# Beginning of a one-core mLSTM / attention / MoE block: per-tile first norm, shared halves, and the products around the router

## What is computed

```python
h = layer_norm(concat([pad, meta, x]), ln_in_g, ln_in_b)
proj = h @ w_in
xm, o_pre, i_pre, f_pre, qa, ka, va, ga, gb = split(proj)
y_m = mlstm_branch(xm, o_pre, i_pre, f_pre, ...)
y_a = diff_attn_branch(qa, ka, va, ...)
merged = sigmoid(ga) * (y_m @ w_branch_m) + sigmoid(gb) * (y_a @ w_branch_a)
h = layer_norm(DN_ALPHA * h + merged @ w_out, ln1_g, ln1_b)
probs = softmax(h @ w_router)
# top group of 4 experts, then top 2 experts in it, weights w normalised
for e in range(16):
    y += combine[:, e:e+1] * ((silu(h @ w_gate[e]) * (h @ w_up[e])) @ w_down[e])
h = layer_norm(DN_ALPHA * h + y, ln2_g, ln2_b)
```

## Time and profile before

| what | value |
|---|---|
| median of three runs | 827.0 us (826.32, 827.0, 827.8) |
| profiled execution, its own time | 827.67 us |
| its span | 825.9 us |
| PE busy in the span | 774.0 us (94%) |
| DVE, ACT, POOL busy | 358.1, 240.7, 25.3 us |
| HBM read | 249.91 MB, 304 GB/s over the span |

### The profile page before, as it was taken

One profiled execution on the slowest core, in us unless ns is written; L12 is line 12 of the kernel. 1 busy time (PEld: TensorE's weight loads), 2 busy tenths in 40 slices (PEclk: granted clock), 3 DMA queues, 4 the chain that ended last, 5 costly groups with the idle time before them and its releaser, 6 DMA issues.

```text
span 825.9 us, 12669 instructions
## 1 busy us (share of the span) xinstructions
PE 774.0 (94%) x4496; PEld 470.1 (57%) x4497; DVE 358.1 (43%) x780; ACT 240.7 (29%) x523; POOL 25.3 (3%) x51
## 2 busy tenths in 40 slices
PE   4999999999999999998999999889999999998993
PEld 3998679999889999882333333333333333332330
DVE  6777446654665787735323213220223122311225
ACT  2554423444766655431110111011110111011100
POOL 2003000000001000000000000000000000000001
PEclk9999999999999999989999999999999999999997
DMA  8965050553105334995999999999999999999992
GB/s 255 388 239 204 0 204 2 203 200 134 76 1 204 135 125 160 394 405 207 428 425 430 428 428 427 430 428 428 406 431 428 430 426 428 429 428 426 431 424 94
DMA packets 36764, 251.30 MB, mean 304 GB/s; under 512 B 5921, under 2 KB 13170, under 8 KB 23426
## 3 DMA queue, kind: packets, MB, share of 16 engines
q1 hardware_dynamic: 34416, 250.76, 73.9%
q10 hardware_dynamic: 2322, 0.21, 0.2%
HBM read 249.91 MB, written 1.05 MB: 304 GB/s over the span
## 4 chain that ended last, share of the span: by engine, by line
PE 72%; DMA 18%; DVE 4%; ACT 2%; issue 2%; POOL 1%; SPq 1%; DVEq 0%; POOLq 0%; ACTq 0%
PE ps L1952 27%; DMA raw<-in_w_up_e_dram 9%; DMA raw<-in_w_down_e_dram 9%; PE ps L1617 8%; PE ps L1619 7%; PE ps L1618 7%; PE ps L1905 3%; PE ps L1913 2%; PE ps L1920 2%; PE ps L1673 1%; PE ps L1669 1%; PE ps L1729 1%; PE ps L1868 1%; PE ps L1592 1%; PE ps L1870 1%
## 5 line engine op out<-in xcount | busy, mean ns | idle before, releaser
L1617 PE MATMUL ps<-hi_h,whi 128*128 128x256 f32 (+1 forms) x448 | 129.8, 290 | 3.3 <-DVE wlo L983 3.2
L1619 PE MATMUL ps<-hi_h,wlo 128*128 128x256 f32 (+1 forms) x448 | 127.4, 284 | 0.0
L1618 PE MATMUL ps<-lo_h,whi 128*128 128x256 f32 (+1 forms) x448 | 127.3, 284 | 0.0
L1952 PE MATMUL ps<-raw,hid 128*64 128x512 f32 x512 | 114.3, 596 | 7.8 <-DMA raw<-in_w_down_e_dram 7.1
L1952 PE MATMUL ps<-raw,xg 128*64 128x512 f32 x512 | 115.0, 599 | 6.8 <-DMA raw<-in_w_gate_e_dram 3.1
L983 DVE TENSOR_TENSOR wlo<-raw,whi 128x512 fp32r<-128x512 f32 x144 | 93.4, 690 | 45.3 <-ACT whi L688 42.7
L1617 PEld LDWEIGHTS ps<-hi_h,whi 128*128 128x128 f32 x448 | 84.5, 189 | 7.9 <-DVE wlo L983 4.3
L688 ACT CAST whi<-raw 128x512 fp32r<-128x512 f32 (+1 forms) x144 | 83.2, 618 | 13.2 <-PE ps L1619 11.9
L1544 DVE TENSOR_TENSOR gs<-ps,gsig 128x512 f32<-128x512 f32 x16 | 11.1, 691 | 173.9 <-ACT gsig L930 173.1
L1619 PEld LDWEIGHTS ps<-hi_h,wlo 128*128 128x128 f32 x448 | 84.5, 189 | 0.0
L1618 PEld LDWEIGHTS ps<-lo_h,whi 128*128 128x128 f32 x448 | 84.4, 188 | 0.0
(11 more groups left out here) (321 smaller groups left out, 1015.3 us busy)
## 6 DMA issues: line engine op xcount, KB each, us to landing
raw<-in_w_down_e_dram SPq DMA_DIRECT2D x32, 2048.0 KB, 18.4
raw<-in_w_gate_e_dram SPq DMA_DIRECT2D x16, 2048.0 KB, 22.1
raw<-in_w_up_e_dram SPq DMA_DIRECT2D x16, 2048.0 KB, 24.3
gate_x<-in_w_gate_e_dram SPq DMA_DIRECT2D x16, 2048.0 KB, 20.7
raw<-in_w_in_dram SPq DMA_DIRECT2D x28, 1024.0 KB, 9.1
up_x_right<-in_w_up_e_dram SPq DMA_DIRECT2D x16, 1024.0 KB, 27.2
...
raw<-in_w_branch_m_dram SPq DMA_DIRECT2D x4, 1024.0 KB, 8.3
```

The costliest lines, as they stand in the source:

```text
L1617: mm(o, w1, hi[:, k, c0:c0 + n], start=(k == 0), stop=False)
L1618: mm(o, w1, lo[:, k, c0:c0 + n], start=False, stop=False)
L1619: last = mm(o, w2, hi[:, k, c0:c0 + n], start=False, stop=(k == KB - 1))
L1952: last = mm(ps[r0:r0 + SLOTS, bank_no, :], lhs[:, k % 4, k // 4, :], w[:, k % 2, 512 * c:512 * c + 512], start=(k == 0), stop=(k == KB - 1))
```

## The change

On SP, the short loads (`wif`, gate biases, gain and bias by slot, lambda vectors) that ACT issued in the beginning stand on SP's queue, behind the four XM quarters and ahead of `rows_in` and the OG weights; the wait for the first XM quarter there is gone. Sixteen loads of 512 bytes fill a block-diagonal tile `diag` ahead of the "out" weights, after POOL has zeroed it. On POOL, rstd is made for tiles 0 and 1, then for tile 2. On ACT, tile 1 is normalised there, the narrow masks are made first, the odd k of `hfull` are made there, and `wif` is split behind the XM stream. On DVE, tiles are taken one after another, the even k of `hfull` stay, with four buffers, and the `wif` and lambda work also stands behind the XM stream. The residual's four steps come one block later. On PE, 16 fills stand ahead of the transposes, and XM's first block waits for `lo_h` k by k. In the router, the logit products take 128 columns (the 16 router columns eight times), four products of 512 columns replace the 16 of 128, and fills are 2, 4 and 3 in three places instead of 10 in one. Some tiles (`rt`, `mask`, `passed` and others) have other addresses. The hunks stand in the order SP, POOL, ACT, DVE, PE.

```diff
         sp.wait_ge(s.x_in1, 16)
         for m, what in enumerate(MATRICES):
             if what == OG:
-                sp.wait_ge(raw_in[0][0], 16)
+                with nc.allow_non_contiguous_dma(reason="a few short vectors"):
+                    sp.dma_start(wif[:], w_in[0, :, 2048:2056].rearrange("(k p) c -> p k c", p=P)).then_inc(s.wif_in, 16)
+                    sp.dma_start(gate_bias[:, 0:1], b_i.rearrange("a h -> h a")).then_inc(s.gb_in, 16)
+                    sp.dma_start(gate_bias[:, 1:2], b_f.rearrange("a h -> h a")).then_inc(s.gb_in, 16)
+                    for tile, v in ((gain4, ln1_g), (bias4, ln1_b)):
+                        sp.dma_start(tile[:], v[0].rearrange("(c i a) -> i c a", c=2, a=4)).then_inc(s.gain4_in, 16)
+                for j, v in enumerate((lam_q1, lam_q2, lam_k1, lam_k2)):
+                    sp.dma_start(lamv[:, j, :], v[0].partition_broadcast(P)).then_inc(s.lam_in, 16)
                 for j, v in enumerate((ln_in_g, ln_in_b)):
                     sp.dma_start(rows_in[:, j, :], v.partition_broadcast(P)).then_inc(s.rows_in_in, 16)
...
+            if what == "out":
+                sp.wait_ge(s.diag_zero, 2)
+                for r0, v in ((0, ln1_g), (32, ln1_b)):
+                    for k in range(KB):
+                        sp.dma_start(diag[r0 + k:r0 + k + 1, P * k:P * k + P], v[0:1, P * k:P * k + P]).then_inc(s.diag_in, 16)
...
+        pool.wait_ge(s.var_ready, 2)
+        pool.tensor_tensor(rstd[:, 0:2], ve[:, 0:2], minus_half[:, 0:2], ALU.pow).then_inc(s.rstd_ready, 1)
         pool.wait_ge(s.var_ready, 3)
-        pool.tensor_tensor(rstd[0:META, 0:1], ve[0:META, 0:1], minus_half[0:META, 0:1],
-                           ALU.pow).then_inc(s.rstd_ready, 1)
-        pool.tensor_tensor(rstd[:, 1:3], ve[:, 1:3], minus_half[:, 1:3], ALU.pow).then_inc(s.rstd_ready, 1)
+        pool.tensor_tensor(rstd[:, 2:3], ve[:, 2:3], minus_half[:, 2:3], ALU.pow).then_inc(s.rstd_ready, 1)
...
+        pool.wait_ge(s.s_done, AH)
+        pool.memset(diag[:], 0.0).then_inc(s.diag_zero, 1)
+        pool.memset(row_sel[:], 0.0).then_inc(s.diag_zero, 1)
+        pool.wait_ge(s.diag_zero, 2)
+        pool.memset(row_sel[0:KB, 0:1], 1.0).then_inc(s.diag_zero, 1)
+        pool.memset(row_sel[32:32 + KB, 1:2], 1.0).then_inc(s.diag_zero, 1)
+        pool.wait_ge(s.diag_zero, 4)
...
-        with nc.allow_non_contiguous_dma(reason="a few short vectors"):
-            for tile, v in ((gain4, ln1_g), (bias4, ln1_b)):
...
-        for k in range(KB):
-            act.wait_ge(s.h_full, k + 1)
-            act.copy(hi_h[:, k, :], hfull[:, k % 2, :]).then_inc(s.h_hi, 1)
+        act.wait_ge(s.consts, 1)
+        for narrow, wide in ((ident_b, ident), (late_b, late), (ahead_b, ahead), (before_b, before)):
+            act.copy(narrow[:], wide[:]).then_inc(s.masks_ready, 1)
+        act.wait_ge(s.nmr0_ready, 1)
+        act.activation(xt[:, 1, :], xt[:, 1, :], ACT.Identity, bias=nmr0[:], scale=rstd[:, 1:2]).then_inc(s.x1_ready, 1)
...
+        def full_half(k):
+            act.wait_ge(s.ht_t, k + 1)
+            if k >= HB:
+                act.wait_ge(s.h_lo, k - HB + 1)
+            act.activation(hfull[:, k % HB, :], ps[:, 4 + k % 4, 0:S], ACT.Identity, bias=chan[:, C_LNB + k:C_LNB + k + 1],
+                           scale=chan[:, C_LNG + k:C_LNG + k + 1]).then_inc(s.h_odd, 1)
+        def high_half(k):
+            act.wait_ge(s.h_odd if k % 2 else s.h_even, k // 2 + 1)
+            act.copy(hi_h[:, k, :], hfull[:, k % HB, :]).then_inc(s.h_hi, 1)
+        act.wait_ge(s.chan_ready, 1)
+        for k in range(0, KB, 2):
+            full_half(k + 1)
+            high_half(k)
+            high_half(k + 1)
+        stream(XM, OG)
         act.wait_ge(s.wif_in, 16)
...
         act.copy(wif_hi[:, :, 0:MH], wif[:, :, MH:2 * MH]).then_inc(s.wif_split, 1)
         act.copy(wif_hi[:, :, 32:32 + MH], wif[:, :, 0:MH]).then_inc(s.wif_split, 1)
-        stream(XM, OG)
         act.wait_ge(s.lam_sum, 1)
         act.activation(lams[:, 2:4], lams[:, 0:2], ACT.Exp).then_inc(s.lam_exp, 1)
...
+        rows = (META, P, P)
+        def tile_stats(j):
+            n = rows[j]
             dve.wait_ge((s.x_in0, s.x_in1, s.x_in2)[j], 16)
             for c in range(2):
                 own(dve.bn_stats(stats[0:n, j, c, :], xt[0:n, j, 512 * c:512 * c + 512]))
...
+        def tile_mean(j):
+            own(dve.bn_aggr(mv[0:rows[j], j, :], stats[0:rows[j], j, :, :]))
+        def tile_var(j):
+            dve.tensor_scalar(ve[0:rows[j], j:j + 1], mv[0:rows[j], j, 1:2], EPS, None, ALU.add).then_inc(s.var_ready, 1)
+        def tile_norm(j):
+            n = rows[j]
             dve.tensor_scalar(xt[0:n, j, :], xt[0:n, j, :], mv[0:n, j, 0:1], rstd[0:n, j:j + 1],
                               ALU.subtract, ALU.mult).then_inc(s.xn_ready, 1)
+        tile_stats(0)
+        tile_stats(1)
+        own.settle()
+        tile_mean(0)
+        tile_mean(1)
+        own.settle()
+        dve.wait_ge(s.consts, 1)
+        tile_var(0)
+        tile_var(1)
+        tile_stats(2)
+        dve.wait_ge(s.rstd_ready, 1)
+        dve.scalar_tensor_tensor(out=nmr0[:], in0=mv[:, 1, 0:1], scalar=-1.0, in1=rstd[:, 1:2], op0=ALU.mult,
+                                 op1=ALU.mult).then_inc(s.nmr0_ready, 1)
+        own.settle()
+        tile_mean(2)
+        own.settle()
+        tile_var(2)
+        tile_norm(0)
         dve.wait_ge(s.rows_t, 1)
-        dve.tensor_copy(chan[:], ps[:, 7, 0:81]).then_inc(s.chan_ready, 1)
+        dve.tensor_copy(chan[:], ps[:, 3, 0:81]).then_inc(s.chan_ready, 1)
+        dve.wait_ge(s.rstd_ready, 2)
+        tile_norm(2)
         dve.wait_ge(s.chan_ready, 1)
         own(dve.tensor_scalar(chan[:, C_AG:C_AG + 1], chan[:, C_AG:C_AG + 1], 1.0 - LAM_INIT, None, ALU.mult))
+        def full_half(k):
+            dve.wait_ge(s.ht_t, k + 1)
+            dve.tensor_scalar(hfull[:, k % HB, :], ps[:, 4 + k % 4, 0:S], chan[:, C_LNG + k:C_LNG + k + 1],
+                              chan[:, C_LNB + k:C_LNB + k + 1], ALU.mult, ALU.add).then_inc(s.h_even, 1)
         def low_half(k):
             dve.wait_ge(s.h_hi, k + 1)
-            dve.tensor_tensor(lo_h[:, k, :], hfull[:, k % 2, :], hi_h[:, k, :].bitcast(F32),
+            dve.tensor_tensor(lo_h[:, k, :], hfull[:, k % HB, :], hi_h[:, k, :].bitcast(F32),
                               ALU.subtract).then_inc(s.h_lo, 1)
-        for k in range(KB):
-            dve.wait_ge(s.ht_t, k + 1)
-            if k >= 2:
-                dve.wait_ge(s.h_lo, k - 1)
-            dve.tensor_scalar(hfull[:, k % 2, :], ps[:, k % 4, 0:S], chan[:, C_LNG + k:C_LNG + k + 1],
-                              chan[:, C_LNB + k:C_LNB + k + 1], ALU.mult, ALU.add).then_inc(s.h_full, 1)
-            if k:
-                low_half(k - 1)
-        low_half(KB - 1)
...
+        full_half(0)
+        full_half(2)
+        for k in range(0, KB, 2):
+            low_half(k)
+            low_half(k + 1)
+            if k + HB < KB:
+                dve.wait_ge(s.h_lo, k + 1)
+                full_half(k + HB)
         def residual(blk, odd):
-            n = blk - 2
+            n = blk - 3
             if n not in range(2 * TT):
                 return
             t, add = n % TT, n // TT
                 dve.wait_ge(s.hres_scaled, t + 1)
                 dve.tensor_tensor(hres[:, t, :], hres[:, t, :], rows_in[:, 1, :], ALU.add).then_inc(s.hres_ready, 1)
             else:
-                dve.wait_ge(s.xn_ready, t + 2)
+                dve.wait_ge(s.xn_ready, 2)
+                dve.wait_ge(s.x1_ready, 1)
                 dve.tensor_tensor(hres[:, t, :], xt[:, t + 1, :], rows_in[:, 0, :], ALU.mult).then_inc(s.hres_scaled, 1)
         stream(XM, OG, residual)
+        dve.wait_ge(s.wif_split, 2)
+        for a, b in ((0, MH), (32, 0)):
+            own(dve.tensor_tensor(wif_lo[:, :, a:a + MH], wif[:, :, b:b + MH],
+                                  wif_hi[:, :, a:a + MH].bitcast(F32), ALU.subtract))
+        own.settle()
+        dve.sem_inc(s.wif_split, 1)
+        dve.wait_ge(s.lam_in, 64)
+        own(dve.tensor_tensor(lamp[:], lamv[:, 0:2, :], lamv[:, 2:4, :], ALU.mult))
+        own.settle()
+        dve.tensor_reduce(lams[:, 0:2], lamp[:], AX.X, ALU.add).then_inc(s.lam_sum, 1)
+        dve.wait_ge(s.masks_ready, 4)
...
-        pe.transpose(ps[:, 7, 0:81], crow[:], ident[0:81, 0:81]).then_inc(s.rows_t, 1)
-        pe.wait_ge(s.xn_ready, 3)
+        pe.transpose(ps[:, 3, 0:81], crow[:], ident[0:81, 0:81]).then_inc(s.rows_t, 1)
+        keep_warm(2, 16)
+        pe.wait_ge(s.xn_ready, 2)
+        pe.wait_ge(s.x1_ready, 1)
         for k in range(KB):
             if k >= 4:
-                pe.wait_ge(s.h_full, k - 3)
+                pe.wait_ge(s.h_odd if k % 2 else s.h_even, (k - 4) // 2 + 1)
             c = slice(P * k, P * k + P)
-            pe.transpose(ps[:, k % 4, 0:META], xt[0:META, 0, c], ident[0:META, 0:META])
-            pe.transpose(ps[:, k % 4, META:META + P], xt[:, 1, c], ident[:])
```

(35 more changed lines are left out.)

104 lines of the change are left out of this document (46 added, 58 removed).

## The result

The median of four executions went from 827.4 us (826.32 to 832.14) to 817.95 us (816.67 to 819.34); the ratio is 0.9875, 95% interval 0.9832 to 0.9918. Taken from the 827.0 us that I reckoned with, the ratio gives 816.7 us, where I had forecast 819.5 with a range from 817.3: faster, as forecast, but by more than the range allowed. The miss is 0.6 us, less than the interval of the ratio leaves open (813.1 to 820.2 us). The ratio is that of the two means, 817.98 and 828.32 us, and the execution of 832.14 alone lifts the second: without it the mean is 827.04, the ratio about 0.989, and 817.9 us would lie within the range.

What follows compares the result with a forecast made beforehand. The end was taken to follow the first expert unit at a fixed time, with PE the long pole before it. 5.4 - 1.5 + 3.6 = 7.5 us gain gave 819.5 us against the 827.0 median; range 817.3 to 823.5.

Steps and rivals of the forecast that it cites:

- What bounds the kernel: Whole kernel: the end lies a fixed time behind the first expert unit; the DMAs' empty stretch shrinks by nearly 4 us.
- The beginning: Before XM's second block: early fills, faster transposes and work shared with ACT gain 5.4 us, bounds 3.6 and 6.0.
- Behind the XM stream: Between the last XM block and second OG split: moved wif and lambda steps lose 1.5 us, bounds 0.7 and 2.2.
- SP's queue: Loads in the beginning: nine short loads delay the OG weights by up to 5.4 us; taken as no loss.
- (c): OG weights land late behind the short loads, 1 to 2 us of PE wait at 41 us: 821.0; chance 0.08.
- (d): Short loads hold SP's queue, PE loses 9 us or more at the OG weights: 828.5 or later; chance 0.04.
- The router: Logits to rank product: wide products and fewer fills gain 3.6 us if TensorE's clock stays high; bounds -0.1 and 4.3.
- Behind the ranks all is as before: After the rank product: pick, gather and first expert unit stay unchanged; no gain or loss counted.
- may do so again: First expert unit's products, at 0.50 granted clock at 375 us before, may run low again; no time counted.
- Rival (a): Router: the clock falls all the same, gain 0 to 0.6 us instead of 3.6: 822.8; chance 0.14.
- Rival (b): Beginning: the clock falls during the transposes behind the early fills, cost 1.7 us: 821.2; chance 0.16.
- Rival (e): Fills low until 14.2 us, block 1 only 3.6 us earlier, clock also falls at router: 824.9; chance 0.08.

Runs made afterwards that it cites:

- the second profile: Profiled execution of the changed kernel, run again without any edit beside the kernel before: 816.50 us.
- the first experiment: The changed kernel run again without any edit, beside the kernel before on one chip: 816.50 to 819.89 us, ratio 0.9847.

## Why the prediction was right, and where it was wrong

**What bounds the kernel: right.** The end follows the first expert unit at a fixed distance, 443.6 us before and after. The empty stretch of the DMAs was to shrink by nearly 4 us; it went from about 372 to 381 us to about 368.3 to 373.

**The beginning, 5.4 us: right in size, by some luck.** XM's second block starts at 20.16 us, forecast 20.2, before 25.71: 5.5 us. Errors inside cancel. The fills began at 6.85 us, not 7.4, and took 6.21 us, not 5.6, so that they ended at 13.0 us as forecast; in the second profile they ended at 12.1. The three transposes of a k took 0.53 us, not 0.41, since they start 0.16, 0.16 and 0.21 us apart and not 0.135, and all 24 took 4.1 us, not 3.2. But the first block's eight k then followed each other at 0.38 us, as if all halves had been there, where I had PE wait for `lo_h` until 19.7; and the second block followed the first without a gap, where I had it wait for the split of its weights. In the second profile it starts at 19.20 us, 6.5 us earlier than in the profile of before, past my bound of 6.0.

**Behind the XM stream, -1.5 us: right.** Measured -1.7 (54.7 against 53.0 us), of which the steps inside the stream give 1.4 back in one profile.

**SP's queue, 0: right.** The OG weights are issued from 20.28 us and land in 13.0 us; no engine waits for them. The price of the issues was too low: the first two short loads took 2.83 and 3.39 us on the queue, and all nine 9.2 us, not 5.4. It cost nothing. Rivals (c) and (d) fall.

**The router, 3.6 us: right in kind, too small.** The first half's logits start 3.76 us earlier than before (355.11 and 351.35), the rank product 8.44: 4.7 us, past my upper bound of 4.3. Set back by those 3.76 us, the spreading starts at 360.28, where I had the logits end at 360.85, and the mask is written at 364.16, where I had it at 364.7: the wide logits took 2.05 against 1.96 us, and the idle time ahead of them was filled. From its start to the fills the spreading took 3.43 us, not 3.6; four fills held the rank product up for 0.89, not 1.1. That is 0.95, and the last 0.1 I had rounded away (3.6 for 3.7). I had priced records by their full duration, where the pace is the distance between two starts. And the reason was named too broadly: I credited dense, wide products and the filled gap together. With the fills in place neither width alone does anything, and in one profile the two fills in the wait for `ht` and six fills fewer behind the spreading do nearly all of it; whether the fills do it without a wide product in every execution stays open.

**The step that failed.** In the sum it is the router term, 3.6 us where 4.7 were measured. In the range it is another: "Behind the ranks all is as before". I took the one profiled execution of before for the kernel, and priced nothing for executions that differ from it. The arithmetic of my low end was wrong too: the three bounds as I wrote them down give 6.0 - 1.2 + 4.3 = 9.1 us and 817.9; with the bound of 0.7 that I had given for the XM stream they give 9.6 and 817.4. So 817.3 left out nothing as unlikely together; it was all of them together, and the time came out below.

What the runs show in its place is a clock that does three things that vary between executions of one kernel: how long the early fills run low (4.47 to 5.95 us for all of them in the old beginning, 5.29 to 6.39 in the new), where it falls at the router (without the two fills 12.5, 14.1 or 15.65 us from turn to rank product), and whether the gate products run low (7.09 or 8.46 to 8.78 us). The terms of the sum, compared profile with profile (827.67 and 819.34, both with low gate products), give 8.3 us against 7.5. From there to the 10.3 us of the ratio it is 2.0 us. Of these, 1.3 come from the one of four executions before in the group near 832, which the router's fills abolish. The other 0.7 come from the executions after that are faster than the profiled one (816.67 and 817.03 us), less the same before: by the two profiles of the changed kernel such an execution has the gate products at full clock (1.6 us) and shorter early fills (1.0 us). In the first experiment, where nine of 17 executions of before are in the upper group, the ratio was 0.9847. The earlier trace rows showed two of these falls; that the second need not come ("may do so again", I wrote) had a price of 1.4 us, and it belonged in the range, below the forecast.

**Rival (a)**, the clock falls at the router all the same, did not happen in any profile with the two fills; without them, in the kernel with the new beginning alone, it did, 10 us long. In eight executions of the kernel before with the two fills it may have (their mean clock says so). **Rival (b)**: the clock did not fall behind the early fills. **Rival (e)** did not come either: the fills ended at 13.3 us at the latest. The Trainium skill, "TensorE: Matmul & The Clock Gate", Part 4, PE-mode transpose, says that transposes don't count as busy for the clock gate in the way that products do. The traces agree as far as they don't raise it: 24 of them in a row, without fills, ran at 421 and 474 ns to the last, and before as well. But 24 transposes in 4.1 us right behind the fills did not let it fall either, and the first XM products took 289 to 299 ns in the mean. The 1.7 us that I had put on this rule were not paid in any profile.

**What stays open.** I saw the upper group of before in one profile only; that all its executions look so is inferred from their times. The upper group of the kernel with two fills, near 828.3, was not seen in a profile, and it is the larger one: eight of twelve executions. Why the clock rises earlier or later within the same fills, and why the gate products fall low in one execution and not in the next, no run shows. Whether the early fills could be fewer was not tried.
